# Two-layer hybrid transformer block on one core: the mixer's conditioning rows, the centring, the key offsets and the softplus moved to other engines and places

## The chip, the core and the metric

The kernel runs on one core of a Trainium2 chip. A core has a matrix engine (TensorE, PE in the rows), a vector engine (VectorE, DVE), an activation engine (ScalarE, ACT), a general engine (GpSimd, POOL) and a queue engine (SyncE, SP) that here only starts the loads of the weights. Each engine runs its own instruction list in order and waits on semaphores. The metric is device time of the whole program in microseconds (us), lower is better.

## What is computed

A first block of two layers and a second block of two layers on 256 tokens of width 1024, all in 32-bit floats. The change touches the first block only. Cut to what matters:

```python
def first_block(x, c, ada_w, ada_b, ...):
    for l in range(DEPTH):                       # DEPTH = 2
        mod = (jax.nn.silu(c) @ ada_w[l] + ada_b[l]).reshape(bsz, 3, 3, 1, D_MODEL)
        u = modulate(h, mod[:, 0, 0], mod[:, 0, 1])
        y = swiglu_ffn(u, ...)
        h = layer_norm(DN_ALPHA * h + MACARON_WEIGHT * mod[:, 0, 2] * y, ...)
        u = modulate(h, mod[:, 1, 0], mod[:, 1, 1])
        y = hybrid_token_mixer(u, w_in[l], ...)
        h = layer_norm(DN_ALPHA * h + mod[:, 1, 2] * y, ...)
        ...                                      # second swiglu_ffn, with mod[:, 2, :]

def hybrid_token_mixer(u, w_in, ...):
    a_in, b_in, c_in, g_in = _split(u @ w_in, ...)
    y_a = conformer_conv(a_in, ...) @ w_a_out    # 31-tap causal conv, layer norm, silu
    y_b = mamba2_ssd(b_in, ...) @ w_b_out        # 4-tap conv, silu, dt = softplus(dt + bias), scan
    y_c = nsa_attention(c_in, ...) @ w_c_out     # rope, compressed keys (kv + pe) @ w1, selection
    return (g0 * y_a + g1 * y_b + g2 * y_c) @ w_o
```

The nine vectors of `mod` are the conditioning. Each is one row `silu(c) @ ada_w` of 1024 numbers, and costs the read of a 1024x1024 matrix (4 MB). The mixer's own gate and the next modulation need three of them: `mod[40:48]`, `mod[48:56]` and `mod[56:64]` in the kernel's column layout.

## The kernel before

Each engine has its own program, written out by hand (`tensor1`, `scalar1`, `vector1`, `gpsimd1` for the first block); no scheduler moves anything. Weights come in chunks of 128x1024 (512 KB) through a ring of nine buffers. A chunk is split in two parts: ACT copies it to the rounded part (`high`, L1025, three buffers, so chunk i waits for the products of chunk i-3), then DVE (L1385, L1440) or POOL (L1850, L1855) subtracts to get the rest (`ring_parts`, called low), and PE does three products per tile (L429 to L431), 24 per chunk in the mixer. In the mixer's front, chunks `C_MIX` to `C_CK` (69 of them: GLU 16, XBC 16, Z 8, small 1, Q 8, KC, VC, KS, KW, VS, VW 2 each, GA 8), all lows are POOL's.

A conditioning row of the mixer works like this. POOL starts eight 512 KB loads (`load_later`, L1831, each after the buffer's last reader); `modulation_rows` (L482) is 32 products of 32 columns on PE, one wait for a load per four; ACT keeps the row (L1103), `modulation_columns` (L494) turns it with two transposes, and DVE adds the bias in `keep_mixed`. The three rows stand after the products of GLU pair 1, GLU pair 4 and XBC pair 0.

On DVE the mixer is one list: `glu` of the first four channel tiles, the 31-tap convolution on tiles 0 to 3 (`conv`, four instructions a tap, sums in PSUM, a drain after each tap; the other four `glu` between taps), `keep_mixed`, the same on tiles 4 to 7, then the 4-tap convolution on 16 tiles in four groups, with the centring of the first convolution's norm behind the second of them, the 32 offset additions of the compressed keys (`kpe`, L1572), the norm's scaling (L1429, L1577), rope of q (L1589 to L1592) and of k (L1597 to L1600), and, much later, `log1p` and what follows it up to the signal `dtv` (L1897 to L1628), for which PE's L738 waits. The mean over the first convolution is PE's L529 behind Q pair 3. PE computes the eight GA chunks, then eight pairs of key products (L696, L697; the n-th waits for n rope signals), then the compressed keys (L708), which wait for `kpe` and the ninth rope signal.

```python
            if n == 3:
                t.wait_ge(sem["aconv"], at("aconv", 4))
                accumulate_ones(0, m.ac, "aconv", 0, con("mean")).then_inc(sem["mu"], 1)
```

## Time and profile before

| | |
|---|---|
| median of 3 runs | 2846.19 us |
| lowest, highest | 2838.16, 2848.96 us |
| the profiled execution's own time | 2837.41 us |
| its span, first to last instruction | 2835.7 us |
| PE busy | 2666.4 us (94%) |
| DVE, ACT, POOL busy | 1773.6 (63%), 1180.1 (42%), 963.0 us (34%) |
| chain that ended last | PE 82%, DVE 8%, ACT 3%, POOL 2%, DMA 2% |

The busy time is from one profiled execution. The chain that ended last follows the work back from the last instruction, at each step to what released it; its shares say on which engine time must be saved. The four layers follow one another; the first block's mixers stand at about 258 to 700 us and 1221 to 1660 us. A row of the timeline has the start in us from the span's start, the duration in us, the engine, the line, the operation, out<-in, a count, and in brackets the idle time before it and what ended it. A fp32 product is recorded as two, so x16 can be eight products. Starts are the safe thing to subtract.

### The profile page before, as it was taken

Reading aid. Unit: us, or ns where it says so; the run is one execution under the profiler, and the core shown is the slowest. Engines: PE = TensorE matmul, PEld = TensorE weight load, DVE = VectorE, ACT = ScalarE, POOL = GpSimd, SP = SyncE. Lnnn points to the kernel's source line nnn. Section 1 sums busy time; section 2 is a strip of 40 time slices with the busy share of each in tenths; the row PEclk is TensorE's granted clock in tenths of the full one; section 3 lists DMA queues with packets and bytes.
Section 4 is the critical chain, followed back from the end, with each engine's and each line's share of the span. In section 5 each row is a group of like instructions: output and inputs, shape, how many; then the busy total and the mean of one; then the engine's idle time right before and its main releaser. Section 6 shows DMA issues by size and latency. Waiting matters only on the chain.

```text
span 2835.7 us, 51763 instructions
## 1 busy us (share of the span) xinstructions
PE 2666.4 (94%) x19971; PEld 2493.8 (88%) x19976; DVE 1773.6 (63%) x2830; ACT 1180.1 (42%) x1981; POOL 963.0 (34%) x524
## 2 busy tenths in 40 slices
PE   4999999899999999989998999998988999988999
PEld 3998899778889989979996888998977999977899
DVE  6763698456375685649955653775554576555576
ACT  2444345235244454434442542444442444442444
POOL 2434775100033333368640000332640244540244
PEclk9999999899999999999998999999999999999999
DMA  8765654323367576566432225763433455333454
GB/s 321 264 211 205 252 167 129 105 90 107 123 243 246 180 254 241 179 246 226 152 127 75 98 90 191 258 229 124 135 97 112 155 186 170 125 107 104 149 185 134
DMA packets 131493, 481.38 MB, mean 170 GB/s; under 512 B 14848, under 2 KB 14848, under 8 KB 130560
## 3 DMA queue, kind: packets, MB, share of 16 engines
q1 hardware_dynamic: 107280, 389.12, 41.6%
q0 software_dynamic: 23040, 83.90, 8.0%
q10 hardware_dynamic: 1008, 6.06, 0.6%
q8 instruction: 116, 1.90, 0.3%
q14 instruction: 49, 0.40, 0.0%
HBM read 475.87 MB, written 3.15 MB: 169 GB/s over the span
## 4 chain that ended last, share of the span: by engine, by line
PE 82%; DVE 8%; ACT 3%; POOL 2%; DMA 2%; DVEq 1%; issue 1%; SPq 0%; ACTq 0%
PE ps L429 19%; PE ps L431 19%; PE ps L430 18%; PE ps L681 5%; PE ps L2167 2%; PE ps L979 2%; PE ps L529 2%; POOL ring_parts L1850 2%; DMA qr<-ada_dram 1%; PE ps L439 1%; PE ps L440 1%; PE ps L438 1%; PE ps L2133 1%; PE ps L471 1%; PE ps L899 1%
## 5 line engine op out<-in xcount | busy, mean ns | idle before, releaser
L430 PE MATMUL ps<-u_parts,high 128*128 128x256 f32 x3712 | 1061.2, 286 | 0.0
L430 PEld LDWEIGHTS ps<-u_parts,high 128*128 128x128 f32 x3712 | 716.9, 193 | 2.0
L1025 ACT ACTIVATE high<-ring 128x1024 fp32r<-128x1024 f32 x437 | 460.6, 1056 | 447.7 <-PE ps L431 347.8
L429 PE MATMUL ps<-ac_parts,high 128*128 128x256 f32 x1920 | 549.5, 286 | 24.1 <-DVE u_parts L1407 13.7
L431 PE MATMUL ps<-ac_parts,ring_parts 128*128 128x256 f32 x1920 | 546.6, 285 | 0.0
L429 PEld LDWEIGHTS ps<-ac_parts,high 128*128 128x128 f32 x1920 | 367.4, 191 | 30.4 <-issue 21.5
L1855 POOL TENSOR_TENSOR ring_parts<-ring,high 128x1024 fp32r<-128x1024 f32 x88 | 224.9, 2556 | 491.9 <-ACT high L1025 491.9
L429 PE MATMUL ps<-h_parts,high 128*128 128x256 f32 x1296 | 380.5, 294 | 11.2 <-DVE u_parts L1407 8.1
L1850 POOL TENSOR_TENSOR ring_parts<-ring,high 128x1024 fp32r<-128x1024 f32 x138 | 333.1, 2420 | 170.0 <-ACT high L1025 168.0
L431 PE MATMUL ps<-h_parts,ring_parts 128*128 128x256 f32 x1296 | 373.2, 288 | 0.0
L431 PEld LDWEIGHTS ps<-ac_parts,ring_parts 128*128 128x128 f32 x1920 | 366.0, 191 | 0.0
L1385 DVE TENSOR_TENSOR ring_parts<-ring,high 128x1024 fp32r<-128x1024 f32 x176 | 217.8, 1239 | 216.6 <-ACT high L1025 192.7
L429 PE MATMUL ps<-pt_parts,high 128*128 128x256 f32 x1216 | 342.1, 281 | 1.5 <-DVE pt_parts L1455 1.5
L430 PE MATMUL ps<-pt_parts,high 128*128 128x256 f32 x1216 | 340.2, 280 | 0.0
L431 PE MATMUL ps<-pt_parts,ring_parts 128*128 128x256 f32 x1216 | 340.2, 280 | 0.0
L2638 POOL TENSOR_TENSOR ring_parts<-ring,high 128x1024 fp32r<-128x1024 f32 x64 | 153.6, 2400 | 381.0 <-ACT high L2227 380.9
L2227 ACT ACTIVATE high<-ring 128x1024 fp32r<-128x1024 f32 x195 | 206.1, 1057 | 182.8 <-PE ps L431 115.2
L429 PEld LDWEIGHTS ps<-h_parts,high 128*128 128x128 f32 x1296 | 253.2, 195 | 26.4 <-issue 20.9
L431 PEld LDWEIGHTS ps<-h_parts,ring_parts 128*128 128x128 f32 x1296 | 253.0, 195 | 1.0
L1831 POOL DMA_DIRECT2D xc<-ada_dram x72 | 39.1, 544 | 611.2 <-DVE u L1398 586.2
L431 PEld LDWEIGHTS ps<-pt_parts,ring_parts 128*128 128x128 f32 x1216 | 231.4, 190 | 0.0
L429 PEld LDWEIGHTS ps<-pt_parts,high 128*128 128x128 f32 x1216 | 228.5, 188 | 2.1 <-DVE pt_parts L1455 2.1
(409 smaller groups left out, 4996.8 us busy)
## 6 DMA issues: line engine op xcount, KB each, us to landing
ring<-stream_dram SPq DMA_DIRECT2D x736, 512.0 KB, 3.5
xc<-ada_dram POOLq DMA_DIRECT2D x80, 512.0 KB, 6.2
z<-ada_dram POOLq DMA_DIRECT2D x40, 512.0 KB, 7.1
qr<-ada_dram POOLq DMA_DIRECT2D x40, 512.0 KB, 8.7
h_aside<-ac ACTq DMA_DIRECT2D x2, 1024.0 KB, 8.0
h<-h_aside ACTq DMA_DIRECT2D x2, 1024.0 KB, 5.7
conb<-con_dram ACTq DMA_DIRECT2D x1, 1088.0 KB, 6.5
h<-x_t_dram SPq DMA_DIRECT2D x1, 1024.0 KB, 5.4
```

The lines of the kernel that those rows point to most:

```text
L429: mm(out, hi, xh, start=start, stop=False, **kw)
L430: mm(out, hi, xl, start=False, stop=False, **kw)
L431: return mm(out, lo, xh, start=False, stop=stop, **kw)
L529: last = mm(ps[:, bank, 0:S], ones, src[:, n], start=n == 0, stop=n == ND - 1)
L681: last = mm(out, chunk_tile(m, i, k), src[:, k], start=k == 0, stop=k == 7)
L979: last = mm(ps[:, unit(j), 0:S], chunk_tile(m, C_WO + n, k), m.merged[:, k], start=k == 0, stop=k == 7)
L1025: act(high_of(m, i), chunk_of(m, i), ACT.Copy).then_inc(made, 1)
L1385: tt(low_of(m, i), chunk_of(m, i), high_of(m, i), ALU.subtract).then_inc(sem["lo"], 1)
L1850: nc.gpsimd.tensor_tensor(low_of(m, i), chunk_of(m, i), high_of(m, i), ALU.subtract)\
L1855: nc.gpsimd.tensor_tensor(low_of(m, i), chunk_of(m, i), high_of(m, i), ALU.subtract)\
L2227: act(high_of(m, i), chunk_of(m, i), ACT.Copy).then_inc(sem["hi"], 1)
L2638: nc.gpsimd.tensor_tensor(low_of(m, i), chunk_of(m, i), high_of(m, i), ALU.subtract)\
```

## The change

Four moves, in the first block only.

1. Conditioning rows. The first of the three is computed by PE right behind the first norm's sums, and its loads start already in the third round of the feed-forward loop. The other two leave PE: DVE multiplies and adds each 128x1024 tile into PSUM (`mix_group`), eight instructions between taps of each 31-tap convolution, the last one writing to SBUF; 16 products of one column (`con("ones", 1)`) on PE, beside the `dtt` products, sum the partitions. Their loads are started by POOL between its lows. `affine` moves to head 3 of the scan.
2. Centring. The mean stands behind Q pair 5 and the centring on DVE behind one conv group instead of two.
3. The 32 `kpe` additions move from DVE to POOL, behind its last low of the front.
4. `dtexp` on ACT and `log1p` to `dtv` on DVE move ahead, to just behind the scaling of the norm.

```diff
+    m.ada_late = m.ada[0:4] + [eb[:, 0:1024], eb[:, 1024:2048]] + m.ada[0:2]
+    m.ada_mixed = [cmp_[:, 0:1024], cmp_[:, 1024:2048]]
...
         layer_norm((0,), m.h, m.u, 4, 5, ("resid", 0))
+        modulation_rows(t, mm, m, ada, ada.group(l, 1))
...
-            if n in (1, 4):
-                modulation_rows(t, mm, m, ada, ada.group(l, 1, n // 3))
-            elif n in (2, 5):
-                t.wait_ge(ada.rows, l * 3 + n // 3 + 1)
-                modulation_columns(nc, m, n // 3)
+            if n == 2:
+                t.wait_ge(ada.rows, l + 1)
+                modulation_columns(nc, m).then_inc(ada.mixed, 1)
...
-            if n == 0:
-                modulation_rows(t, mm, m, ada, ada.group(l, 1, 2))
-            elif n == 1:
-                t.wait_ge(ada.rows, l * 3 + 3)
-                modulation_columns(nc, m, 2).then_inc(ada.mixed, 1)
...
-            if n == 3:
-                t.wait_ge(sem["aconv"], at("aconv", 4))
+            if n == 5:
+                t.wait_ge(sem["aconv"], at("aconv", 5))
...
+        for n in range(2):
+            for k in range(8):
+                last = mm(ps[:, unit(j), P + 8 * n + k:P + 8 * n + k + 1], m.ada_mixed[n][:, k * P:(k + 1) * P],
+                          con("ones", 1), start=True, stop=True)
         last.then_inc(sem["dtt"], 1)
...
             act(m.ac[:, n], m.ac[:, n], ACT.Silu, scale=par("ag", n), bias=par("abb", n)).then_inc(sem["anorm"], 1)
+        act(m.dtw[:, 0], m.dtraw, ACT.Abs)
+        act(m.aexp[0:16], par("alog")[0:16], ACT.Exp)
+        a.drain()
+        act(m.dtw[:, 1], m.dtw[:, 0], ACT.Exp, scale=-1.0).then_inc(sem["dtexp"], 1)
...
+        def mix_group(it, k, bank_):
+            g = ada.group(l, 1, it)
+            tile = (m.ada, m.ada_late)[it - 1][k]
+            sums = ps[:, bank_:bank_ + 2, :]
+            wide = lambda t: t.rearrange("p (b n) -> p b n", b=2)
+            c = m.cvec[:, k:k + 1]
+            v.wait_ge(ada.landed[k], 16 * (g + 1))
+            if k == 0:
+                last = ts(sums, wide(tile), c, None, ALU.mult)
+            else:
+                last = stt(sums if k < ND - 1 else wide(m.ada_mixed[it - 1]), wide(tile), c, sums, ALU.mult, ALU.add)
+            last.then_inc(ada.used, 1)
...
+        def beside_first(k):
+            if k in (3, 5, 7, 9):
+                glu(4 + (k - 3) // 2)
+            elif k >= 12 and k % 2 == 0 and k < 28:
+                mix_group(1, (k - 12) // 2, 2)
+        late = (2, 4, 6, 8, 10, 12, 16, 20)
+        def beside_second(k):
+            if k in late:
+                mix_group(2, late.index(k), 0)
...
+        for n in (0, 4, 8, 12):
             v.wait_ge(sem["copied"], at("copied", n // 2 + 2))
             conv(m.xc, m.xpad, "xw", "xb", TAPS_B, n, 2, "xconv")
+            if n == 0:
+                centre(1, m.ac, 0, 8)
...
         for n in range(ND):
             tt(m.ac[:, n], m.ac[:, n], m.rs, ALU.mult).then_inc(sem["anrs"], 1)
+        v.wait_ge(sem["dtexp"], at("dtexp", 1))
+        log1p(nc, v, m.dtw[:, 1], m.dtw[:, 0], m.dtw[:, 2], m.dtw[:, 3], m.dtw[:, 4])
...
         v.wait_ge(sem["dtt"], at("dtt", 1))
+        tt(m.mod[:, 48:64], ps[:, bank(j), P:P + 16], par("ada_b", 48, 16), ALU.add)
...
-            with g.Fori(0, 2) as it:
+            with g.Fori(0, 3 if q == 0 else 2) as it:
...
+        def load_late(k):
+            if k < 6:
+                g.wait_ge(ada.used, second * ND + k + 1)
+            else:
+                g.wait_ge(ada.used, third * ND + k - 5)
+            g.dma_start(m.ada_late[k], ada_source[third * ND + k]).then_inc(ada.landed[k], 16)
+        late = {20: 0, 22: 1, 24: 2, 26: 3, 27: 4, 29: 5, 35: 6, 37: 7}
         for n, i in enumerate(range(C_MIX, C_CK)):
             low(i)
+            if 3 <= n < 7:
+                load_later(second, 2 * (n - 3))
+                load_later(second, 2 * (n - 3) + 1)
+            elif n in late:
+                load_late(late[n])
+        g.wait_ge(ada.used, (third + 1) * ND)
+        for b, (src, pe) in enumerate(((m.kc, "pek"), (m.vc, "pev"))):
+            g.wait_ge(sem["copied"], at("copied", 18 + b))
+            for q in range(16):
+                last = nc.gpsimd.tensor_scalar(...)
+            last.then_inc(sem["kpe"], 1)
```

How the instructions stand, at three places. DVE between the 4-tap convolution and rope of q (`xc` the 4-tap result, `ac` the normed one, `eb` the offset keys, `pt` and `kv` the softplus work tiles). Before:

```order
L1552 SCALAR_TENSOR_TENSOR xc<-xp,par,ps 128x256 x4
L1572 TENSOR_SCALAR eb<-kv,par 128x60 x32
L1429 RECIPROCAL st<-st 128x256
L1577 TENSOR_TENSOR ac<-ac,st 128x256 x8
L1589 TENSOR_TENSOR sg<-ps,conb 128x512
```

After:

```order
L1555 SCALAR_TENSOR_TENSOR xc<-xp,par,ps 128x256 x4
L1420 RECIPROCAL st<-st 128x256
L1581 TENSOR_TENSOR ac<-ac,st 128x256 x8
L1922 TENSOR_SCALAR pt<-pt 16x256
L1924 RECIPROCAL pt<-pt 16x256
L1926 TENSOR_TENSOR pt<-pt 16x256
L1928 TENSOR_TENSOR pt<-pt 16x256
L1930 TENSOR_SCALAR pt<-pt 16x256
L1933 SCALAR_TENSOR_TENSOR pt<-pt 16x256 x6
L1935 SCALAR_TENSOR_TENSOR pt<-pt 16x256
L1937 TENSOR_SCALAR pt<-pt 16x256
L1600 TENSOR_TENSOR sg<-ps,conb 128x512
```

The 32 additions are gone from DVE, and the softplus stands ahead of rope (three more of its instructions are left out of the rows). POOL from the start of the mixer's front to the end of it (`ring_parts<-ring,high` is a low, DMA a conditioning load), after:

```order
L1857 TENSOR_TENSOR ring_parts<-ring,high 128x1024 x4
L1838 DMA xc<-ada_dram 128x1024 x2
L1857 TENSOR_TENSOR ring_parts<-ring,high 128x1024
...
L1838 DMA qr<-ada_dram 128x1024 x2
L1857 TENSOR_TENSOR ring_parts<-ring,high 128x1024 x14
L1894 DMA xc<-ada_dram 128x1024
...
L1857 TENSOR_TENSOR ring_parts<-ring,high 128x1024 x31
L1909 TENSOR_SCALAR eb<-kv,par 128x60 x32
```

Before, its first loads of the front stood behind the seventh low and the list ended with the lows; the additions are new at its end. PE behind the first norm, before:

```order
L529 MATMUL ps<-u,con 128x256 x8
L429 MATMUL ps<-h_parts,high 128x256
L430 MATMUL ps<-u_parts,high 128x256
L431 MATMUL ps<-h_parts,ring_parts 128x256
```

After:

```order
L526 MATMUL ps<-u,con 128x256 x8
L485 MATMUL ps<-xc,cvec 32x256 x16
L485 MATMUL ps<-z,cvec 32x256 x8
L485 MATMUL ps<-qr,cvec 32x256 x8
L432 MATMUL ps<-h_parts,high 128x256
```

The first conditioning row now stands between the norm's sum and the first GLU chunk.

## Rows read from the trace of the kernel before

**Rows 1.** Waits of PE: line <- releaser: us in total, times, longest us

```profile
PE ps L738 <- DVE kv L1628: 13.8, 2, 6.9
PE ps L482 <- DMA qr<-ada_dram: 9.8, 6, 1.9
```

**Rows 2.** Timeline of PE, first mixer: start, us, engine, line [idle <- releaser]

```profile
258.47 0.55 PE L429 MATMUL ps<-h_parts,high 128*128 128x256 f32 x1 [4.07 <-DVE u_parts L1407]
...
273.50 1.93 PE L482 MATMUL ps<-xc,cvec 128*32 128x256 f32 x32
...
277.09 0.38 PE L429 MATMUL ps<-h_parts,high 128*128 128x256 f32 x1
...
294.76 1.93 PE L482 MATMUL ps<-xc,cvec 128*32 128x256 f32 x32
...
303.76 0.58 PE L429 MATMUL ps<-h_parts,high 128*128 128x256 f32 x1
...
329.77 1.93 PE L482 MATMUL ps<-xc,cvec 128*32 128x256 f32 x32
...
335.15 0.38 PE L429 MATMUL ps<-h_parts,high 128*128 128x256 f32 x1
```

**Rows 3.** Stretches of 3 us: PE busy (instructions), granted clock, DMA share, GB/s

```profile
258.00:261.00 3.00, 2.53 (x12) 0.50 0.72 298
...
303.00:306.00 3.00, 3.00 (x18) 0.50 0.00 0
...
549.00:552.00 3.00, 2.70 (x10) 0.50 0.00 0
```

**Rows 4.** Timeline of POOL, first instructions and first mixer

```profile
0.42 0.10 POOL L2862 MEMSET const-float32-1.0<- 128x1 f32 x1
...
267.99 2.39 POOL L1850 TENSOR_TENSOR ring_parts<-ring,high 128x1024 fp32r<-128x1024 f32 x1 [15.45 <-ACT high L1025]
...
280.98 1.09 POOL L1831 DMA_DIRECT2D xc<-ada_dram  x2
...
348.80 4.86 POOL L1850 TENSOR_TENSOR ring_parts<-ring,high 128x1024 fp32r<-128x1024 f32 x2 [0.90 <-ACT high L1025]
...
492.39 8.04 POOL L1850 TENSOR_TENSOR ring_parts<-ring,high 128x1024 fp32r<-128x1024 f32 x3 [3.75 <-ACT high L1025]
```

**Rows 5.** Timeline of DVE, both mixers

```profile
417.96 1.66 DVE L1552 SCALAR_TENSOR_TENSOR ac<-ap,par,ps 128x256 f32<-128x256 f32 x4
...
495.87 2.29 DVE L1590 TENSOR_TENSOR qr<-qr,conb 128x512 f32<-128x512 f32 x1
...
541.92 2.85 DVE L1908 SCALAR_TENSOR_TENSOR kv<-kv 16x256 f32<-16x256 f32 x6
...
1420.05 4.91 DVE L1572 TENSOR_SCALAR eb<-kv,par 128x60 f32<-128x60 f32 x3
...
1424.88 2.27 DVE L1572 TENSOR_SCALAR eb<-kv,par 128x60 f32<-128x60 f32 x12
```

**Rows 6.** Timeline of ACT, first mixer

```profile
491.00 0.36 ACT L1176 ACTIVATE pt<-ps 128x256 f32<-128x256 f32 x1
...
529.16 1.28 ACT L1195 ACT_TABLE_LOAD   x1
530.45 0.20 ACT L1195 ACTIVATE small<-par 16x1 f32<-16x1 f32 x1
```

**Rows 7.** Timeline of PE: one-column sums of the loop, then the mixer's second half

```profile
106.82 1.84 PE L471 MATMUL ps<-con,eb 128*128 128x1 f32 x16
...
487.32 0.47 PE L429 MATMUL ps<-h_parts,high 128*128 128x256 f32 x1
...
517.57 2.67 PE L708 MATMUL ps<-eb,ring 128*128 128x60 f32 x22
...
547.03 1.86 PE L738 MATMUL ps<-con,kv 16*128 16x16 f32 x8 [6.89 <-DVE kv L1628]
...
552.06 3.20 PE L765 MATMUL ps<-con,xc 128*128 128x128 f32 x16
```

More of the change, by code:

```diff
@@ L1098, in layer @@
         high_u(1, m.uhi)
-        def modulation_kept(n):
-            a.wait_ge(ada.used, ND * (ada.group(l, 1, n) + 1))
-            act(m.ada_rows[n], ps[:, 2, 0:S], ACT.Copy).then_inc(ada.rows, 1)
         j = 0
@@ L1111, in layer @@
             act(m.sg[:, n % 4], ps[:, bank(j if n > 0 else 3), S:2 * S], ACT.Sigmoid).then_inc(sem["sg"], 1)
-            if n in (1, 4):
-                modulation_kept(n // 3)
+            if n == 0:
+                a.wait_ge(ada.used, ND * (ada.group(l, 1) + 1))
+                act(m.ada_rows, ps[:, 2, 0:S], ACT.Copy).then_inc(ada.rows, 1)
             later_high(C_GLU + 2 * n + 4)
@@ L1191, in layer @@
         j += 3
-        act(m.dtw[:, 0], m.dtraw, ACT.Abs)
-        act(m.aexp[0:16], par("alog")[0:16], ACT.Exp)
-        a.drain()
-        act(m.dtw[:, 1], m.dtw[:, 0], ACT.Exp, scale=-1.0).then_inc(sem["dtexp"], 1)
         act(m.gate_a[:], m.gate_a[:], ACT.Sigmoid).then_inc(sem["outsg"], 1)
@@ L1538, in layer, with conv @@
             glu(n)
-        v.drain()
-        def conv(dst, src, w, b, taps, lo, bank_, signal, between=()):
+        keep_mixed()
+        def conv(dst, src, w, b, taps, lo, bank_, signal, beside=lambda k: None):
             sums = lambda n: ps[:, bank_ + (n - lo) // 2, (n - lo) % 2 * S:(n - lo) % 2 * S + S]
@@ L1553, in conv @@
                             .then_inc(sem[signal], 1)
[L1554 to L1555 removed]
+                beside(k)
                 v.drain()
         v.wait_ge(sem["aside"], at("aside", 16))
[L1559 to L1562 removed]
+        def beside_first(k):
[7 more added lines that the diff above has]
+                mix_group(2, late.index(k), 0)
+        conv(m.ac, m.apad, "aw", "ab", TAPS_A, 0, 0, "aconv", beside_first)
+        conv(m.ac, m.apad, "aw", "ab", TAPS_A, 4, 2, "aconv", beside_second)
+        for n in (0, 4, 8, 12):
             v.wait_ge(sem["copied"], at("copied", n // 2 + 2))
             conv(m.xc, m.xpad, "xw", "xb", TAPS_B, n, 2, "xconv")
[L1565 to L1574 removed]
+            if n == 0:
+                centre(1, m.ac, 0, 8)
         inverse_root(1)
@@ L1619, in layer @@
         j += 1
-        v.wait_ge(sem["dtexp"], at("dtexp", 1))
-        log1p(nc, v, m.dtw[:, 1], m.dtw[:, 0], m.dtw[:, 2], m.dtw[:, 3], m.dtw[:, 4])
-        ts(m.dtw[:, 0], m.dtraw, 0.0, None, ALU.max)
-        v.drain()
-        tt(m.dtw[:, 3], m.dtw[:, 3], m.dtw[:, 0], ALU.add)
-        v.drain()
-        ts(m.dtw[:, 4], m.dtw[:, 3], m.aexp[0:16], -1.0, ALU.mult, ALU.mult).then_inc(sem["dtv"], 1)
         def add_branch(branch, n, y, chunk):
```

61 lines of the change are left out of this document (22 added, 39 removed).

## The prediction

> **What bounds the kernel now.** I read the table of engines first: PE is busy 94% of the span and carries 82% of the chain that ended last, so only time in which PE waits, works at half clock or does work that can leave it is worth anything. Then PE's waits, where the change aims at two: for the conditioning loads, 9.8 us before the last two tiles alone, and 13.8 us for `dtv`, twice 6.9 [rows 1]. Then PE's timeline through one mixer [rows 2, 7], the granted clock in short stretches [rows 3], and what POOL, DVE and ACT do beside it [rows 4 to 6]. The reader should see that after two of PE's pauses the clock is 0.50, the 1.2 GHz level, for some 6 us [rows 3]. All below is for the first layer; the second differs by 1 to 2 us.
>
> **Part 1, the conditioning rows on PE.** The three groups of 32 narrow products hold PE from 273.50 to 277.09, 294.76 to 303.76 and 329.77 to 335.15 [rows 2]: 3.6 + 9.0 + 5.4 = 18.0 us, of which 3.6 each is work and the rest waits for loads. With two of three pairs of transposes 18.3 us leave the stretch. The one group that stays on PE goes into the 4.07 us in which PE waits for the norm [rows 2]; its loads start a loop round earlier, where the loop's first two rounds already carry the same loads. So it costs nothing; without that cover it would cost 3.6.
>
> **The clock.** Six chunks took 277.09 to 294.76, so 2.92 each [rows 2]. The four ahead of 273.50 took 15.0 us instead of 11.7, at 0.50 [rows 2, 3]. With PE busy in the pause the clock should stay up; about 1 us stays lost, as the first chunk follows DVE's input rows and the fourth a low, so 2.3 come back. The eight chunks from 303.76 to 329.77 took 26.0 instead of 23.4 and the transposes [rows 2, 3], the price of the load waits: 2.4 come back.
>
> **POOL in the front.** A low takes 2.39 us, two load starts 1.09 [rows 4]: together 3.5, over PE's 2.92 a chunk. Before, the first of these starts fell behind the seventh low, where PE was itself held by its narrow products. Now they stand behind lows 4 to 7, with PE at full speed, and each delays the next low; by chunk 8 PE is 2.2 us behind. The late loads come singly and find 0.90 us of POOL idle per two chunks [rows 4]. The seventh waits for DVE's first late tile; by my count it finds POOL 0.5 us early and PE 1.7 us away from feeling it. So part 1 gives 18.3 + 2.3 + 2.4 - 2.2 = 20.8 in the first layer, some 18 to 19 in the second, whose waits were shorter: **20 per layer**.
>
> **DVE beside the convolution.** No row shows a 1024-column instruction into PSUM. From below, four times a 256-column tap would give 1.7 (1.66 for four [rows 5]), from above nothing over a blocked 2.3 [rows 5]; scaled by columns with one fixed cost it is 1.23. I take 1.23: 16 are 20 us. Against that `keep_mixed` loses its 4 us of small steps, and the later `glu` tiles no longer hold DVE, since PE no longer stops. Before, the convolution ended at 419.6 [rows 5]; I get 419.8. PE reaches its mean at 422.3, two Q pairs later in the list but 20.8 us earlier in time. The margin is 2.5 us, cost nothing. The centring needs the mean at 425.7 and DVE is there at 427. The four conv groups end near 451 and nothing waits for them before PE's GA chunks at 466.
>
> **ACT at the GA chunks.** `dtexp` costs Abs, a table load of 1.28 and two exponentials, 2.4 us, and a second table load before the next Silu [rows 6]. It stands ahead of the first GA copy, for which GA chunk 2 waits. Copy and high come 2.4 to 3.7 us later than at 491.00 [rows 6], and the lows of GA 3 and 4 follow. Counting chunk by chunk, PE ends the GA chunks 1.9 us late. The Trainium skill (ScalarE: Activation LUTs, What ACT_TABLE_LOAD costs) adds a drain of 1.38 us to each load. In this trace the activation starts 0.01 us behind the load's end (530.45 after 529.16 + 1.28 [rows 6]), so I add none; by the page PE would lose up to 2.8 us more per layer.
>
> **The softplus in POOL's busy stretch.** This is where most of the gain goes. A DVE instruction that reads two SBUF operands, or a small one-operand one, does not run beside a POOL subtraction: L1590 took 2.29 us, and the key offsets went three in 4.91 us beside POOL's lows but twelve in 2.27 us without them [rows 5]. The Trainium skill names the shared interface and these two kinds of instruction (GPSIMD Engine Reference, 1. Specifications); the rows agree. In the GA stretch POOL's lows stand back to back, three in 8.04 us [rows 4]. Before, the softplus ran with POOL idle: six steps in 2.85 us [rows 5]. Its steps are separated by drains, so beside lows about one gets through per low, 2.7 us each. Counted from the first GA chunk: `dtexp` at 6.1; the first two steps by 8.2; then one step a low until POOL's last low ends at 21.9, with eight steps left. From there POOL runs the 32 offset additions and DVE gets in between them.
>
> The price of one addition on POOL has no row. The nearest are a 128x1 memset, 0.10 us, and a load start, 0.54 [rows 4]; 60 columns at the rate of a low are 0.14. I take 0.25, nearest to memset plus columns, and keep 0.14 to 0.54. Then the eight steps take 5.3 us (to 27.2), rope of q 9.4 (to 36.6) and five ropes of k 6.9: PE may start the compressed keys at **43.5**. Before it did at 517.57 - 487.32 = 30.25 [rows 7]. Loss 13.2, the 1.9 of ACT included. With 0.14 it is 10, with 0.54 21, where POOL's additions end last. PE idles through that stretch in small pieces and comes out at half clock, as it did behind 4.07 us of waiting: **3.0** more.
>
> **Around `dtv`.** From the end of the last branch product, 547.03 - 6.89 = 540.14, to 552.06 were 11.9 us [rows 7], the end of it at 0.50 [rows 3]. Now the wait is gone, 16 one-column products are added at 1.84 / 8 = 0.23 each [rows 7], 3.7 us, the four `dtt` products take 0.9, DVE's two small steps 0.6, the five scan products 1.4 at 2.4 GHz: 6.4. **Gain 5.5**; at half clock throughout nothing. `affine` at head 3 falls into DVE's idle time.
>
> **Sum.** 20 - 13.2 - 3.0 + 5.5 = 9.3 per layer, 18.6 for two. The profiled execution's own time, 2837.4, becomes 2818.8. It lies 8.8 under the median of 2846.2, so against the median 2827.6, **2828 us**. The bounds of one addition give 25 and 3 us instead of 19: 2821 to 2843.
>
> **Rivals.**
> (a) *The softplus is not held.* If 16-partition steps pass beside POOL's lows, or several per low, it is done at 14.6 and rope keeps ahead of PE but for 0.5 us. For: the rows of blocked instructions all have 128 partitions. Against: it is one interface. Per layer 20 - 1.9 - 0.5 + 5.5 = 23, with the rest two layers give 46: **2800**.
> (b) *The additions on POOL are slow* (the other side). One mechanism: a fixed cost per instruction on POOL, before PE's compressed keys. 32 of them must fit beside DVE's steps between 21.9 and 34; from 0.65 us each the whole change gives nothing, and at 1.0 PE loses 31 instead of 13.2: 20 - 31 - 3 + 5.5 = -8.5 per layer, **2863**. For: POOL's only short rows are a memset and load starts. Against: a low's 2.39 us leaves little fixed cost beside its 1024 columns. The Trainium skill (GPSIMD Engine Reference, 7. Performance pitfalls) charges 2.9 cycles an element for steps over 8 bytes, as here; that would be an estimated 0.15 us, near my lower end.
> (c) *The conditioning on DVE comes late.* If half of POOL's lows hold the 1024-column steps by 1.2 us each, DVE is 19 us late and PE's mean waits 16: **2859**. Against: the taps, one SBUF operand and PSUM, kept 0.42 us beside POOL (four in 1.66 [rows 5]).
> (d) *The front gives only half*: the clock falls in the pause all the same, or POOL's starts cost more. 10 instead of 20, and the rest as forecast, -0.7 per layer: about **2848**.
>
> **Chances.** Forecast 0.55, (a) 0.20, (b) 0.08, (c) 0.05, (d) 0.12. Half a per cent, 14 us, is what a measurement of this kernel can tell from no change. Of the forecast's share 0.42 lies over 14 us of gain, the rest under; (a) is all faster, (d) all the same, (b) and (c) slower. Faster 0.62, same 0.26, slower 0.12. The range takes in (a), with some us below it for its own spread, and (d): 2794 to 2850.
>
> **What would show it.** Right: PE's row behind the norm without 4 us of idle and at full clock; no wait of PE for loads; DVE's 16 steps near 1.23 us; softplus steps over 2 us beside lows; PE waiting some 11 us in each mixer for rope or `kpe` ahead of the compressed keys, and none for `dtv`. Wrong: softplus steps of 0.4 us throughout (a); PE's wait named POOL with additions of over 0.6 us (b); a wait for `aconv` at the mean (c).

## The result, and the profile of the changed kernel

The changed kernel took **2804.5 us** (median), beside 2843.7 for the kernel before on the same chip: ratio 0.9866, 95% interval 0.9850 to 0.9882. That is 39 us faster; the forecast was 18.6, with 2828 us inside a range of 2794 to 2850. One of the changed kernel's four executions took 3452 us at a mean granted clock of 0.71; it is in the median and not in the ratio, and the other three took 2802 to 2806. The profiled executions differ by less: 2837.4 before, 2803.4 after, 34.1 us. The kernel before went from 2838 to 2849 in the other executions, so its profiled one is at the low end. All steps below are made on the profiles.

Waits of PE (line <- releaser: us in total, times, longest). The two rows of [rows 1] are gone. New is the wait for the ropes, `qr`.

```profile
PE ps L432 <- DVE u_parts L1398: 14.7, 6, 5.6
...
PE ps L687 <- DVE qr L1603: 7.4, 8, 1.5
...
PE ps L432 <- POOL ring_parts L1857: 4.4, 14, 0.4
```

PE's timeline (start, us, engine, line, idle and releaser): the conditioning group in the pause, the first GLU chunk, the first GA product, the first copy product of the rope of k, the compressed keys, the `dtt` and one-column products, the scan, and the first mean product ahead of the second block.

```profile
254.40 1.93 PE L485 MATMUL ps<-xc,cvec 128*32 128x256 f32 x32
...
258.55 0.36 PE L432 MATMUL ps<-h_parts,high 128*128 128x256 f32 x1 [0.48 <-DVE u_parts L1398]
...
466.06 0.47 PE L432 MATMUL ps<-h_parts,high 128*128 128x256 f32 x1
...
492.61 0.70 PE L687 MATMUL ps<-kraw,conb 128*128 128x256 f32 x2 [1.52 <-DVE qr L1603]
...
505.77 1.44 PE L699 MATMUL ps<-eb,ring 128*128 128x60 f32 x12
...
528.17 1.06 PE L729 MATMUL ps<-con,pt 16*128 16x16 f32 x8
529.16 5.28 PE L734 MATMUL ps<-con,cmp 128*128 128x1 f32 x32
...
537.68 3.68 PE L761 MATMUL ps<-con,xc 128*128 128x128 f32 x16
...
1925.75 0.38 PE L526 MATMUL ps<-h,con 128*128 128x256 f32 x1
```

Set against [rows 7] the gain in the first layer grows and shrinks like this: 487.32 - 466.06 = **21.3** at the first GA product, 517.57 - 505.77 = **11.8** at the compressed keys, 547.03 - 528.17 = **18.9** at `dtt`, 552.06 - 537.68 = **14.4** at the scan. The second layer, counted from its own start: 21.4, 13.7, 20.7, 17.4.

Stretches of 3 us (length, PE busy and its instructions, granted clock, DMA share, GB/s): behind the norm, in the wait for the ropes, at the compressed keys, and at the one-column products.

```profile
258.00:261.00 3.00, 2.52 (x23) 1.00 0.00 0
...
498.00:501.00 3.00, 2.34 (x6) 0.50 0.01 3
504.00:507.00 3.00, 3.00 (x21) 1.00 0.03 5
528.00:531.00 3.00, 3.00 (x27) 1.00 0.50 153
531.00:534.00 3.00, 3.00 (x16) 0.51 0.06 22
534.00:537.00 3.00, 2.51 (x11) 0.50 0.00 0
```

The first row answers to the first of [rows 3]: full clock where it was 0.50. DVE: one conditioning step, the centring, the softplus and the first rope.

```profile
318.90 1.28 DVE L1513 SCALAR_TENSOR_TENSOR ps<-xc,cvec,ps 128x1024 f32<-128x1024 f32 x1
...
426.60 2.74 DVE L1416 TENSOR_TENSOR ac<-ac,ps 128x256 f32<-128x256 f32 x8 [0.36 <-PE ps L526]
...
472.17 0.28 DVE L1922 TENSOR_SCALAR pt<-pt 16x256 f32<-16x256 f32 x1 [14.58 <-ACT pt L1167]
...
476.66 0.28 DVE L1930 TENSOR_SCALAR pt<-pt 16x256 f32<-16x256 f32 x1
477.02 11.13 DVE L1933 SCALAR_TENSOR_TENSOR pt<-pt 16x256 f32<-16x256 f32 x6
...
489.57 0.52 DVE L1586 TENSOR_TENSOR pt<-pt 16x256 f32<-16x256 f32 x1
...
490.51 0.67 DVE L1600 TENSOR_TENSOR sg<-ps,conb 128x512 f32<-128x512 f32 x1
```

POOL in the same stretch: its last four subtractions of the front, then the 32 key offset additions.

```profile
476.68 10.18 POOL L1857 TENSOR_TENSOR ring_parts<-ring,high 128x1024 fp32r<-128x1024 f32 x4 [0.86 <-ACT high L1021]
486.93 19.39 POOL L1909 TENSOR_SCALAR eb<-kv,par 128x60 f32<-128x60 f32 x32
```

The reader should see three things. The row of 11.13 us has six steps of the softplus: the first four stood beside the four subtractions and took 2.5 us each, the last two stood beside POOL's first small additions and took 0.43 each, as short as the steps behind them. Before that stretch, 14.58 us of DVE stand empty, since ScalarE's exponentials come behind the norm's activations. And the additions took 19.39 / 32 = 0.61 us each on average, more than the 0.54 that I had as the upper bound.

### The profile page after: what moved, and what is told of

It reads as the page before. It is cut to its first block, busy times and chain, and to the rows that moved or that the text cites. A ratio compares the mean times of both kernels' runs of the same rounds, so it can differ in the third digit from the quotient of the medians.

```text
span 2801.7 us, 51457 instructions
## 1 busy us (share of the span) xinstructions
PE 2654.6 (95%) x19771; PEld 2486.5 (89%) x19776; DVE 1779.5 (64%) x2796; ACT 1181.2 (42%) x1979; POOL 1000.6 (36%) x588
## 4 chain that ended last, share of the span: by engine, by line
PE 84%; DVE 9%; ACT 3%; POOL 1%; DVEq 1%; issue 1%; DMA 0%; SPq 0%; ACTq 0%
PE ps L432 20%; PE ps L434 19%; PE ps L433 19%; PE ps L672 5%; PE ps L2192 2%; PE ps L975 2%; PE ps L526 2%; PE ps L442 1%; PE ps L443 1%; PE ps L441 1%; PE ps L2158 1%; PE ps L474 1%; POOL ring_parts L1857 1%; PE ps L895 1%; DVE pt L1933 1%
## 5 line engine op out<-in xcount | busy, mean ns | idle before, releaser
L432 PE MATMUL ps<-ac_parts,high 128*128 128x256 f32 x1920 | 549.6, 286 | 24.0 <-DVE u_parts L1398 13.7
L432 PEld LDWEIGHTS ps<-ac_parts,high 128*128 128x128 f32 x1920 | 366.7, 191 | 30.0 <-issue 21.6
L432 PEld LDWEIGHTS ps<-h_parts,high 128*128 128x128 f32 x1296 | 248.7, 192 | 20.7 <-issue 11.2
```

Of the source, the lines that this page charges most:

```text
L432: mm(out, hi, xh, start=start, stop=False, **kw)
```

## Experiments

Eleven further kernels were run. The gain is read at one place: 1959.29 (start of the first mean product ahead of the second block, kernel before) minus the start of the same row. The first block's two layers lie before it.

```profile
1959.29 0.38 PE L529 MATMUL ps<-h,con 128*128 128x256 f32 x1
```

| kernel | median us | ratio to before [95%] | gain in the first block | gain in the whole span |
|---|---|---|---|---|
| changed kernel | 2804.5 | 0.9866 [0.9850, 0.9882] | 33.5 | 34.0 |
| m12 | 2799.5 | 0.9861 [0.9832, 0.9890] | 30.5 | 39.5 |
| kp_dve | 2798.3 | 0.9847 [0.9819, 0.9875] | 30.2 | 38.9 |
| late_softplus | 2820.5 | 0.9919 [0.9888, 0.9949] | 15.2 | 15.4 |
| early_exp | 2803.6 | 0.9872 [0.9843, 0.9901] | 36.1 | 36.8 |
| early_exp_kp4 | 2787.2 | 0.9820 [0.9801, 0.9840] | 50.2 | 50.5 |
| early_exp_dve4 | 2789.4 | 0.9814 [0.9784, 0.9843] | 51.2 | 52.1 |
| kp4_late_softplus | 2806.4 | 0.9873 [0.9844, 0.9902] | 31.4 | 31.9 |
| kp4_columns_ga | 2785.1 | 0.9791 [0.9759, 0.9824] | 51.2 | 51.5 |
| columns_early | 2835.9 | 0.9978 [0.9965, 0.9990] | 3.4 | 4.1 |
| combo | 2824.6 | 0.9948 [0.9930, 0.9967] | 10.6 | 14.6 |
| rows_back | 2816.0 | 0.9921 [0.9899, 0.9942] | 22.1 | 22.4 |

### The ladder: which part carries the gain

**m12**, the conditioning and the centring alone:

```diff
-        g.wait_ge(ada.used, (third + 1) * ND)
-        for b, (src, pe) in enumerate(((m.kc, "pek"), (m.vc, "pev"))):
...
-                last = nc.gpsimd.tensor_scalar(m.kp[b][:, q]...
...
+                last = ts(m.kp[b][:, q]...
...
         inverse_root(1)
...
         for n in range(ND):
             tt(m.ac[:, n], m.ac[:, n], m.rs, ALU.mult).then_inc(sem["anrs"], 1)
-        v.wait_ge(sem["dtexp"], at("dtexp", 1))
-        log1p(nc, v, m.dtw[:, 1], m.dtw[:, 0], m.dtw[:, 2], m.dtw[:, 3], m.dtw[:, 4])
...
         last.then_inc(sem["vbc"], 1)
         j += 1
+        v.wait_ge(sem["dtexp"], at("dtexp", 1))
+        log1p(nc, v, m.dtw[:, 1], m.dtw[:, 0], m.dtw[:, 2], m.dtw[:, 3], m.dtw[:, 4])
...
```

> Only the first two parts of the change: conditioning in the norm's pause and on VectorE, centring behind one conv group. The key offsets are on VectorE and the softplus is late, as in the kernel before. Theory A (the front is worth 20 to 21 us per layer and the rest of the change nearly nothing by itself): PE reaches the first GA product 14 to 21 us earlier than before, the wait for dtv of 6.9 us stays, the 16 one-column products add 2 to 4: 12 to 16 us per layer, 2812 to 2820 us. Rival B (the later moves carry a good part of the result): 2825 us or more. Rival C (the front carries all of it and the later moves cost): 2804 us or less.

Measured: 30.5 us in the first block, where theory A had 24 to 32. The first two parts carry nearly all of it, and the two later moves together add 3.0 us. The median, 2799.5, lies in rival C's range and under A's 2812 to 2820; 9 us of it came from the second block, which is told at the end of this section. PE's rows in the first layer:

```profile
495.95 7.36 PE L699 MATMUL ps<-eb,ring 128*128 128x60 f32 x64
...
525.41 1.85 PE L729 MATMUL ps<-con,pt 16*128 16x16 f32 x8 [6.89 <-DVE pt L1636]
527.19 6.99 PE L734 MATMUL ps<-con,cmp 128*128 128x1 f32 x32
```

The compressed keys start 517.57 - 495.95 = 21.6 us earlier: all of the front arrives. Then the wait for `dtv` is there at its full 6.89, and behind it, at half clock, the 16 one-column products take 6.99 us.

**late_softplus**, the changed kernel with part 4 undone:

```diff
         act(m.ac[:, n], m.ac[:, n], ACT.Silu, ...).then_inc(sem["anorm"], 1)
-        act(m.dtw[:, 0], m.dtraw, ACT.Abs)
...
         act(m.kcr, ps[:, bank(j), 0:60], ACT.Copy).then_inc(sem["kcr"], 1)
         j += 3
+        act(m.dtw[:, 0], m.dtraw, ACT.Abs)
...
```

and on VectorE the second half of m12's diff.

> The changed kernel with the softplus put back where it was: ScalarE's two exponentials behind the copy of the raw compressed keys, VectorE's 17 steps behind the copy of the value block. Everything else as changed. Theory A (the softplus is held by GpSimd's subtractions and stands in front of the ropes): without it the ropes run right behind the last GA product, so the compressed keys start about 30 us behind the first GA product instead of 39.7; of these 9.5 us some 0 to 6 are eaten by GpSimd's key offsets, which ended only at 506.3. The wait for dtv of 6.9 us comes back, and the stretch behind it is at half clock. Net 1 to 4 us per layer slower than the changed kernel: 2806 to 2813 us. Rival B (the stall in front of the compressed keys comes from GpSimd's 32 additions, not from the softplus): the compressed keys still start near 39.7 us behind GA, and the wait for dtv is added on top: 6.9 to 10 us per layer slower, 2818 to 2825 us.

Measured: 18.3 us less in the first block than the changed kernel, far over theory A and inside B's 14 to 20. But B's reason is wrong: the compressed keys started at 495.38, 10.4 us earlier than in the changed kernel, as A had it. The stall ahead of them was the softplus. What I had mis-sized was the other side:

```profile
500.13 5.48 PE L699 MATMUL ps<-eb,ring 128*128 128x60 f32 x32 [0.97 <-POOL eb L1909]
529.32 1.00 PE L729 MATMUL ps<-con,pt 16*128 16x16 f32 x4 [6.89 <-DVE pt L1630]
```

With the ropes out of the way PE reaches `kpe` before POOL does. From the compressed keys to `dtt` it takes 33.9 us where m12 takes 29.5, though PE waits only 0.97 of these 4.5; behind the wait the granted clock was 0.65, 0.50 and 0.71 in the stretches from 501 to 510, where m12 has 1.00. The second layer loses 5.1 us in the same way, and another 3.7 in and just behind the short products that follow the scan (L779), which ran at 0.50 there and at 0.89 and 0.68 in m12. Against m12, part 3 alone costs 15.3 us in the two layers.

**kp_dve**, the changed kernel with part 3 undone:

```diff
-        g.wait_ge(ada.used, (third + 1) * ND)
-        for b, (src, pe) in enumerate(((m.kc, "pek"), (m.vc, "pev"))):
...
-                last = nc.gpsimd.tensor_scalar(m.kp[b][:, q]...
...
+                last = ts(m.kp[b][:, q]...
...
         inverse_root(1)
```

> The changed kernel with the 32 key offset additions back on VectorE, ahead of the inverse root. In the kernel before they took 15 us there (three in 4.91 beside lows, twelve in 2.27 without). Theory A: the norm's eight products end at about 472 instead of 457.6, PE waits 4 to 7 us at the first GA product, the softplus starts behind POOL's lows and is quick (0.4 us a step), so compressed keys start 30 to 34 us behind GA instead of 39.7. Net -2 to +3 us per layer: 2800 to 2811 us. Rival B (moving the offsets to GpSimd was the costly part): over 6 us per layer faster, under 2793 us. Rival C (the offsets on VectorE put everything behind them later by their whole 15 us): 2820 us or more.

Measured: 30.2 us in the first block, 3.3 less than the changed kernel, so theory A by the amount, but not by its reason. The norm's products ended at 468.1, ScalarE's exponentials let the softplus begin only at 471.87, as in the changed kernel, and it ran into the same subtractions:

```profile
476.73 5.01 DVE L1932 SCALAR_TENSOR_TENSOR pt<-pt 16x256 f32<-16x256 f32 x2
482.17 5.66 DVE L1932 SCALAR_TENSOR_TENSOR pt<-pt 16x256 f32<-16x256 f32 x4 [0.43 <-issue]
```

The compressed keys started 38.7 us behind the first GA product, not 30 to 34. PE's scan started 2.5 us earlier than in the changed kernel, and 3.6 were lost again in and just behind the short products that follow it, at a clock of 0.50 where the changed kernel has 0.78 and 0.79:

```profile
538.79 7.01 PE L779 MATMUL ps<-small,qr 64*128 64x15 f32 x64
```

There the changed kernel took 3.92. So with the softplus in this place, it is nearly the same where the 32 additions stand, 10.3 us on DVE (451.12 to 461.44) or 19.4 on POOL. The times of m12 and kp_dve are the lower ones for another reason, told at the end of this section.

### The stall ahead of the compressed keys

**early_exp**: ScalarE's exponentials forward, so that DVE finds them in its empty 14.58 us:

```diff
         act(m.dtraw, ps[0:16, bank(j), S:2 * S], ACT.Identity, ...).then_inc(copied, 1)
+        a.drain()
+        act(m.dtw[:, 0], m.dtraw, ACT.Abs)
+        act(m.aexp[0:16], par("alog")[0:16], ACT.Exp)
+        a.drain()
+        act(m.dtw[:, 1], m.dtw[:, 0], ACT.Exp, scale=-1.0).then_inc(sem["dtexp"], 1)
...
```

> The changed kernel with ScalarE's Abs and two exponentials moved forward, right behind the copy of the raw step sizes (small projection). VectorE then has the softplus's input when it comes out of the norm's eight products at 457.6 and can use the 14.6 us in which it now waits. Theory A (the softplus is held by subtractions, about one step per low): it still needs some 20 to 25 us, but ends at 478 to 484 instead of 490.6, so the ropes reach PE right behind the last GA product: compressed keys 31 to 34 us behind the first GA product instead of 39.7, 6 to 8 us per layer gained, 2788 to 2793 us. ScalarE pays two more table loads at the small projection, where PE does not wait for it. Rival B (GpSimd's additions are what the compressed keys wait for): the waits for ropes become one for kpe, and the start stays at 38 to 40: 2803 to 2806 us. Rival C: the two table loads (2.6 us) hold the copies of Q there and PE waits: 1 to 3 us per layer lost of the gain.

Measured: 2803.6, the number of rival B. In the trace all three theories have their part. DVE's softplus ran from 458.68 to 470.49, most steps at 0.3 to 0.4 us and only two held by a subtraction, to 1.74 and 2.43: POOL does not stand back to back there. ScalarE's two table loads do cost PE something (rival C): behind the small projection it waited 0.91 us for a low, and was 1.1 us late from there on, in both layers. The ropes cost PE nothing, and the compressed keys started at 497.56 instead of 505.77, 8.2 us earlier. Then PE met POOL's additions, which ran from 486.07 to 503.15:

```profile
499.73 1.61 PE L699 MATMUL ps<-eb,ring 128*128 128x60 f32 x13
...
503.21 6.07 PE L699 MATMUL ps<-eb,ring 128*128 128x60 f32 x32 [1.86 <-POOL eb L1910]
```

`dtt` came at 525.42, 2.75 earlier: the wait of 1.86 and the half clock behind it took 5.5 of the 8.2. In the changed kernel the softplus's stall covered the slow additions.

**early_exp_kp4**: the same, and 4 additions of 480 elements on GpSimd in place of 32 of 60:

```diff
-            for q in range(16):
-                last = nc.gpsimd.tensor_scalar(m.kp[b][:, q]..., src[:, :, 2 * q:2 * q + 225:16],
...
+            for h in range(2):
+                keys = src[:, :, 16 * h:16 * h + 240].rearrange("p g (n r o) -> p r g n o", n=15, o=2)[:, :, :, :, 0]
...
+                last = nc.gpsimd.tensor_tensor(m.kp[b][:, 8 * h:8 * h + 8]..., keys, pos, ALU.add)
```

> early_exp with the 32 additions of 60 elements on GpSimd replaced by 4 of 480 elements, same values, same place. In early_exp 26 of the 32 took 14.12 us, 0.54 each. Theory A (a fixed cost per instruction): the four take 3 to 6 us together, kpe comes 10 us earlier, PE's wait of 1.9 us at the compressed values and the half clock behind it (3.5 us) go: 5 us per layer under early_exp, 2791 to 2796 us. Rival B (a cost per strided element, 9 ns): the four take 17 us together and hold VectorE's ropes in pieces of 4.3 us: 2803 to 2815 us.

Measured: 2787.2 us, theory A and 4 us better than its range; both kernels of this study are slower. POOL and PE:

```profile
486.04 5.79 POOL L1913 TENSOR_TENSOR eb<-kv,par 128x480 f32<-128x480 f32 x4
```

```profile
497.56 7.36 PE L699 MATMUL ps<-eb,ring 128*128 128x60 f32 x64
...
521.05 3.73 PE L734 MATMUL ps<-con,cmp 128*128 128x1 f32 x32
```

The same 1920 elements take 5.79 us instead of 17.1: 1.45 for 480 and 0.54 for 60 give, solved for two unknowns, an estimated 0.40 us per instruction and 2.2 ns per element, if the two operations cost alike. The keys' products run in one piece, and the first block gains 50.2 instead of 36.1, 7 us a layer where A had 5. Of the rest 1.6 in the first layer are the one-column products, which now end before the clock falls.

**early_exp_dve4**, the same four additions on VectorE (against early_exp_kp4):

```diff
-                last = nc.gpsimd.tensor_tensor(m.kp[b][:, 8 * h:8 * h + 8]..., keys, pos, ALU.add)
...
+                last = nc.vector.tensor_tensor(m.kp[b][:, 8 * h:8 * h + 8]..., keys, pos, ALU.add)
...
         inverse_root(1)
```

> early_exp with the key offsets as 4 additions of 480 elements on VectorE, ahead of the inverse root, in place of 32 on GpSimd. Tells whether GpSimd or the number of instructions was at fault. Theory A (the number): each of the four takes 0.6 to 2.7 us (held by a subtraction or not), the norm's products end 3 to 8 us later than in early_exp_kp4, which PE feels by 0 to 2 us at GA, and everything else is the same: 2786 to 2792 us. Rival B (VectorE's late norm pushes the softplus into GpSimd's busy stretch, so its steps are held again and PE waits for the ropes): 5 us per layer, 2795 to 2801 us.

Measured: 2789.4, theory A. With four additions it makes no difference which engine has them, 51.2 us against 50.2; what had cost was their number:

```profile
452.22 3.70 DVE L1586 TENSOR_TENSOR eb<-kv,par 128x480 f32<-128x480 f32 x4
```

**kp4_late_softplus**: what the place of the softplus is worth once the additions are short:

```diff
-                last = nc.gpsimd.tensor_scalar(m.kp[b][:, q]...
+                last = nc.gpsimd.tensor_tensor(m.kp[b][:, 8 * h:8 * h + 8]..., keys, pos, ALU.add)
```

beside late_softplus's diff.

> The changed kernel with 4 additions of 480 elements on GpSimd and the softplus back at its late place, so that only the place of the softplus differs from early_exp_kp4 (2787.2). Theory A (the softplus's early place is worth the wait for dtv, 6.9 us, and the clock that falls in it, 1.7 at the one-column products and some more behind): 8 to 11 us per layer slower than early_exp_kp4, 2803 to 2809 us. Rival B (with the key offsets out of the way the late place costs no more than its wait less what the shorter ScalarE list gives): 5 us per layer or less, 2797 us or less.

Measured: 2806.4, theory A: 18.8 us in two layers, of which 14.2 are the two waits for `dtv`. The rest is a difference: in the first layer the work behind the wait, at a clock of 0.50, took 4.0 us longer up to the scan, and the compressed keys had started 2.1 us earlier. So the early softplus is worth 9.4 us a layer when DVE is free for it. The changed kernel, whose softplus stands in POOL's busy stretch and whose additions are slow, is only 2.1 us ahead of kp4_late_softplus in two layers.

### The norm's pause

**rows_back**: the one group of rows out of the pause, back behind the second GLU pair:

```diff
         layer_norm((0,), m.h, m.u, 4, 5, ("resid", 0))
-        modulation_rows(t, mm, m, ada, ada.group(l, 1))
...
-            if n == 2:
+            if n == 1:
+                modulation_rows(t, mm, m, ada, ada.group(l, 1))
+            elif n == 2:
...
```

> The changed kernel with PE's one remaining group of conditioning rows taken out of the norm's pause and put behind the second GLU pair, where it was before; the loads start as early as in the changed kernel. Theory A (the pause covers 3.6 us of it and keeps the clock up): the pause of 4.1 us is back, the clock is 0.50 for some 6 us behind it (2.3 us), and the rows cost 3.6 in the open: 5 to 6 us per layer slower, 2813 to 2818 us. Rival B (the clock falls or stays whatever stands in the pause): 3.6 us per layer, 2810 to 2813 us. Rival C (the rows' inputs or the slower start of GLU cost nothing, as VectorE's GLU steps set the pace there): 2803 to 2807 us.

Measured: 11.4 us less in the first block, 5.7 a layer, theory A. PE waited 4.07 us for DVE's input rows again, and the clock was 0.74 and 0.69 in the two stretches from 258 where the changed kernel has 1.00. GLU's lows cost more as well: a single wait for one was 1.3 us in the first layer, where the changed kernel's longest is 0.4.

### The one-column products and the clock

**columns_early**: the 16 products forward, behind the norm's mean square:

```diff
         rms(1, m.sq_a, 1)
+        for n in range(2):
+            for k in range(8):
+                mm(ps[:, 0, S + 8 * n + k:S + 8 * n + k + 1], m.ada_mixed[n][:, k * P:(k + 1) * P],
+                   con("ones", 1), start=True, stop=True)
...
```

> The changed kernel with only the 16 one-column products moved from behind the four dtt products to behind the norm's mean square, their results in the free half of PSUM bank 0, VectorE's addition unchanged in place. Theory A (they let the clock fall: granted clock 0.51 at 531 to 534, full again at 541): the stretch from dtt to the scores shrinks from 9.5 to about 4.0 us if the clock stays up, 5.0 if it falls all the same; the products cost 3.7 at their new place, so 1 to 2 us per layer net, 2800 to 2803 us. Rival B (the new place is one where PE was held anyway, by VectorE's root or ScalarE's activations ahead of GA, and the wait shrinks by as much): 4 to 5.5 us per layer, 2793 to 2797 us. Rival C (a spot of low clock moves with them): no gain, 2803 to 2808 us.

Measured: 2835.9, 30 us slower than the changed kernel, which no theory had (C came nearest). The clock:

```profile
441.00:444.00 3.00, 3.00 (x30) 1.00 0.00 0
444.00:447.00 3.00, 3.00 (x20) 0.66 0.02 5
447.00:450.00 3.00, 3.00 (x16) 0.50 0.00 0
...
483.00:486.00 3.00, 3.00 (x13) 0.50 0.00 0
486.00:489.00 3.00, 3.00 (x9) 0.50 0.55 178
489.00:492.00 3.00, 3.00 (x20) 0.95 0.00 0
```

The one-column products ran from 440.87 to 444.50. Right behind them the granted clock fell to 0.50, the 1.2 GHz level, and stayed there for 42 us, through 192 products of 128 columns and most of the rotations of q, with PE busy 3.00 of 3.00 in every row. It came back about a microsecond before the end of those rotations, which have 256 columns:

```profile
484.85 5.88 PE L663 MATMUL ps<-qr,conb 128*128 128x256 f32 x16
```

The first GA product came only at 490.38, so the next expectation is wrong where it puts the return behind it. In the changed kernel the same 192 products ran at 1.00, 29 in 3 us where here it was 16.

**kp4_columns_ga**: the same move on the faster kernel, to directly ahead of the GA chunks:

```diff
+        for n in range(2):
+            for k in range(8):
+                mm(ps[:, 0, S + 8 * n + k:S + 8 * n + k + 1], m.ada_mixed[n][:, k * P:(k + 1) * P],
+                   con("ones", 1), start=True, stop=True)
         for n in range(8):
             if n == 0:
                 t.wait_ge(sem["xconv"], at("xconv", NXB))
...
```

> early_exp_kp4 with the 16 one-column products moved to directly ahead of the GA chunks, whose products have 256 columns (in columns_early they stood ahead of 192 products of 128 columns, and the granted clock was 0.50 from 446 to 489, back at 0.95 only behind the first GA products). Theory A (the one-column products let the clock fall, and products of 256 columns bring it back soon, of 128 columns not): the clock dips for some 6 us at the first GA chunks and is full behind them, at a price of 3.7 + 3; the stretch from dtt to the scores shrinks from 11.6 to 5.1 us. Net 0 us per layer: 2784 to 2790 us, and above all not 2815. Rival B (moved ahead of the long run of products they hold the clock low until PE next pauses, whatever the products' width): the clock stays at 0.50 through the 24 us of GA chunks and beyond, 10 us per layer or more slower, 2805 us or more. Rival C (the clock does not fall here at all): 3 us per layer faster, 2778 to 2783 us.

Measured: 2785.1, with a first block 1.0 us shorter than early_exp_kp4's. The clock was 1.00 in every stretch from 462 to 486, rival C in this, but the gain was A's: the products cost 3.63 at their new place, and the scan at 526.44 started 1.6 us earlier. The low clock that had stood at `dtt` (0.50 from 525) now comes at 531. So 16 products of one column let the clock fall in one place and not in another. What differs is what follows, products of 128 or of 256 columns, and the moment; these two runs don't tell these apart.

**combo**: early_exp_dve4 and columns_early together; its diff is those of the two.

> The changed kernel with three edits: ScalarE's exponentials of the softplus forward (as in early_exp), the 32 key offset additions as 4 VectorE instructions of 480 elements ahead of the inverse root, and the 16 one-column products forward, behind the norm's mean square, into a free half of a PSUM bank. Read at PE's row of the compressed keys and at the start of the mixer's second half. Theory A (the whole stall in front of the compressed keys and the 5.4 us that the offsets cost in early_exp come from the two moves; the one-column products cost 5.3 us on the path where they stand and nothing in full-clock surroundings beyond 3.7): compressed keys near 496 instead of 505.8, no wait for kpe, scan products 9 to 10 plus 2 to 3 us earlier than in the changed kernel: 11 to 14 us per layer, 2776 to 2784 us. Rival B (GpSimd's subtractions delay the four wide additions and PE waits at the first GA product): 2 to 5 us per layer of it are lost, 2784 to 2794 us. Rival C (the gain comes back as a wait in the second half): 2795 us or more.

Measured: 2824.6. By the number that is C's open range, but no theory had the reason, the same fall of the clock. It is 40.6 us worse in the first block than early_exp_dve4, which is combo without the moved products. So that move costs 20 us a layer on that kernel, and 15 on the changed one (30.1 in two layers).

### An unchanged block, 9 us apart

m12 and kp_dve gained 9.0 and 8.7 us in the second block, which no kernel here touches; combo 4.0, all others under 1. The largest piece that I found is whether a subtraction of POOL catches a step of DVE. The changed kernel first, then m12, at the same place of the second block:

```profile
2054.55 0.16 DVE L2531 TENSOR_TENSOR small<-small,par 128x4 f32<-128x4 f32 x1
2054.79 2.36 DVE L2533 TENSOR_SCALAR small<-small 128x4 f32<-128x4 f32 x1
...
2057.33 2.18 DVE L2541 TENSOR_TENSOR small<-small 128x4 f32<-128x4 f32 x1
...
2059.84 5.32 DVE L2547 TENSOR_SCALAR eb<-eb,small 128x256 f32<-128x256 f32 x4
```

```profile
2058.10 2.26 DVE L2530 TENSOR_TENSOR small<-small,par 128x4 f32<-128x4 f32 x1
2060.44 2.28 DVE L2532 TENSOR_SCALAR small<-small 128x4 f32<-128x4 f32 x1
...
2062.90 0.16 DVE L2540 TENSOR_TENSOR small<-small 128x4 f32<-128x4 f32 x1
...
2063.39 1.14 DVE L2546 TENSOR_SCALAR eb<-eb,small 128x256 f32<-128x256 f32 x4
```

A step of four columns takes 0.16 or 2.3 us, and both kernels have two that are held. But in the changed kernel the four scalings behind them are held as well, 5.32 us instead of 1.14. Set to the start of their second blocks, m12 was 0.2 us behind the changed kernel before this place and 3.6 us ahead at the products that wait for the scalings. The rest of its 9.0 comes in small pieces up to 2480 that I did not trace; kp_dve has the same short scalings, and combo, with 4.0, has them held. Why it came out so in three kernels, each of which has the additions on DVE (but so have the kernel before and early_exp_dve4, which gained 0.9), is open. It means that a difference of 9 us between two of these medians needs the first block's row beside it: by medians m12 looks better than the changed kernel, by the part that was changed it is 3 us worse.

## Why the prediction was half the size

By its steps, per layer, forecast against the first and the second layer:

| step | forecast | layer 1 | layer 2 |
|---|---|---|---|
| part 1, the front | +20 | +21.3 | +21.4 |
| GA to compressed keys | -13.2 | -9.5 | -7.7 |
| half clock behind that stretch | -3.0 | 0 | 0 |
| around `dtv` and the scan | +5.5 | +2.6 | +3.7 |
| sum | 9.3 | 14.4 | 17.4 |

The two losses were forecast too large, by 6.7 and 8.5 us; the gain around `dtv` was forecast too large as well, by 2.9 and 1.8, and hides a part of it.

**The front was right.** 20.8 was worked out for the first layer, 21.3 came; the pause is full ([rows 2] had 4.07 us of idle, now 0.48), the clock stays up, the mean does not wait for the convolution, and a conditioning step on DVE took 1.28 us where 1.23 was forecast. That price needed no scaling: the trace of before has the same instruction with its sums in SBUF, at 1.28 each,

```profile
14.73 4.03 DVE L1333 SCALAR_TENSOR_TENSOR eb<-xc,cvec,eb 128x1024 f32<-128x1024 f32 x3
```

m12 shows that the front's gain reaches the end, and rows_back that the pause is worth 5.7.

**The softplus beside POOL: mechanism right, size wrong.** The step that failed was "then one step a low until POOL's last low ends at 21.9, with eight steps left". The low ended at 20.8, and when the step beside it was through, at 21.1, seven were left. POOL's lows do not stand back to back from the GA chunks on: after one from 473.43 there is a gap of 0.86 to 476.68, and two short steps went through there. The seven then took 3.4 us, not the 5.3 for eight that I got by letting them take turns with the additions. The softplus was done 24.5 us behind the first GA product instead of 27.2, rope of q at 32.9 instead of 36.6, the fifth rope of k at 38.8 and the keys at 39.7 instead of 43.5. The other part of the loss was right: PE ended the GA chunks 1.8 us late, forecast 1.9. late_softplus proves the mechanism, since without the softplus the keys start 10.4 us earlier, and early_exp does it without moving the softplus back. Rival (a) is out: the four steps beside lows took 2.5 us each.

**The half clock was counted in the wrong place.** This is the second step that failed, "comes out at half clock". The clock did fall to 0.50 at 498 to 501, but ahead of the keys, in the wait for the ropes and in the copy products of the ropes of k behind it, and it was at 1.00 when the keys began. From the keys to `dtt` PE took 22.40 us, before 29.46 - 6.89 = 22.57. Ahead of the keys it cost at most an estimated 0.9 us: the ninth rope signal, the fifth rope of k, came at 504.8, and the keys started at 505.77. That is in the 9.5 of the row above; the 3.0 us behind it were not there.

**Around `dtv` the gain was half.** The wait of 6.89 is gone, as forecast. But the 16 products took 5.28 where 16 x 0.23 gave 3.7, since the clock fell during them, and everything behind them up to the scan ran at half clock: 9.5 us from `dtt` to the scan, not 6.4. (The terms that I gave, 3.7 + 0.9 + 0.6 + 1.4, add up to 6.6; the gain would have been 5.3.) At full clock they do take 3.63 to 3.73 (kp4_columns_ga, early_exp_kp4), so the price was right and the clock wrong.

**The price of a GpSimd addition was wrong, and it did not matter here.** 0.25 taken, 0.14 to 0.54 as bounds, 0.61 measured, and 0.51 in late_softplus (16.44 us for 32), where DVE stands idle beside the first twelve. Those start 0.46 us apart; beside DVE's ropes a single one took up to 0.8, once 1.22. By my sum 0.54 would have cost 21 us. It did not, because I let DVE "get in between them" as if the two took turns; in fact DVE's steps of the softplus took 0.3 to 0.5 beside the additions, and PE asked for the second half of the offsets only at 509, after POOL's end at 506.3. That it did not matter here was luck. Rival (b) named the right bottleneck one change too early: early_exp has it. The Trainium skill (GPSIMD Engine Reference, 2.1 Instruction dispatch) puts the software call at tens of cycles per instruction. The two sizes give an estimated 0.40 us here, so some hundreds of cycles at the 1.2 GHz that the page's section 1 gives the engine. The page prices the call alone, and these runs don't show what else is in the 0.40; for a sum like mine the measured one decides.

**What is left**: 1.5 us of the first layer behind its scan, most of it in the second feed-forward, and the 5 us by which the medians differ more than the profiles. Rivals (c) and (d) did not occur: DVE waited for PE's mean, not PE for DVE's convolution, and the front gave all of its 20.

## What to carry to other kernels

Free work goes where the engine that receives it is idle and where no long GpSimd instruction stands beside it: the same small steps of the softplus took 18.3 us of VectorE behind the norm's activations and 11.8 when they began 13.5 us earlier, which brought the compressed keys forward by 8.2 us, and it took only the input's earlier arrival. Look behind a stall before it is removed: the next one (here the slow additions) may stand a few us further on and give most of the gain back. On GpSimd and on VectorE fold many small strided instructions into few: the 32 additions took 17.1 and 10.3 us, four of eight times the width 5.8 and 3.7. And read the granted clock behind an edit as well as the rows of the edit: kp_dve lost behind its scan what it had gained ahead of it.

## What the hardware showed that I had not expected

Sixteen one-column products cost 3.6 us by their rows and 15 us a layer by what followed: the granted clock stood at 0.50 for 42 us with PE busy throughout, in a run of 128-column products that otherwise goes at 1.00. The same 16 products directly ahead of 256-column ones did nothing to the clock (1.00 in every stretch from 462 to 486). Why is open. GpSimd's additions of 60 elements take 0.51 to 0.61 us on average, of which, by the estimate above, the elements are the smaller part. And VectorE's steps beside these additions are hardly longer (0.52 instead of 0.41), whereas beside the subtractions of 1024 columns, 2.5 to 2.6 us each, four steps of 0.43 took 2.46 to 2.48 and ended 0.3 us behind the subtraction's end.
